# One exponential for the sinks of a pair of attention units, and sums by VectorE, on one Trainium2 core

## The reference, cut to what matters

```python
def window_attention(q, k, v, kc, vc, sink):
    ...
    logits = jnp.concatenate([s_win, s_ctx, _sink_column(sink, s_win)], axis=-1)
    p = jax.nn.softmax(logits, axis=-1)
    nw = 3 * BLOCK
    nc = kc.shape[1]
    o = (jnp.einsum('bnhgqk,bnkhd->bnqhgd', p[..., :nw].astype(v.dtype), vw)
         + jnp.einsum('bnhgqc,bchd->bnqhgd', p[..., nw:nw + nc].astype(v.dtype), vc))
```

## Time and profile before

| | us |
|---|---|
| median of 3 runs | 2042.43 |
| lowest and highest of the runs | 2041.19, 2049.43 |
| profiled execution, its time | 2047.0 |
| profiled execution, its span | 2045.2 |
| PE busy in the span | 1948.9 |
| DVE busy | 1232.9 |
| ACT busy | 941.1 |
| POOL busy | 491.1 |

### The profile page before, as it was taken

How to read it: one execution, slowest core, us unless ns; L and a number is a source line. 1 busy time by engine, 2 the same in 40 slices (tenths; PEclk the granted TensorE clock), 3 DMA queues, 4 the chain that set the end, 5 groups by cost and what they waited for, 6 DMA issues and landing times.

```text
span 2045.2 us, 30423 instructions
## 1 busy us (share of the span) xinstructions
PE 1948.9 (95%) x12246; PEld 1722.2 (84%) x12246; DVE 1232.9 (60%) x1914; ACT 941.1 (46%) x1490; POOL 491.1 (24%) x326
## 2 busy tenths in 40 slices
PE   7999898899989999999799999999999899999999
PEld 6899886899977888787588788888877898799999
DVE  4688796778855781653763583354365947676410
ACT  4454445555447333433753542233255454765643
POOL 1301022000000000000444544455510000303887
PEclk9999999899999999999999999999999999999999
DMA  6987472466832212221023244465523233144554
GB/s 234 282 303 257 160 256 74 164 237 217 268 110 87 72 52 72 83 83 62 11 93 111 105 151 148 144 200 201 192 87 103 93 118 131 63 148 153 185 189 151
DMA packets 84636, 299.23 MB, mean 146 GB/s; under 512 B 9992, under 2 KB 13200, under 8 KB 84112
## 3 DMA queue, kind: packets, MB, share of 16 engines
q1 hardware_dynamic: 64512, 231.76, 32.9%
q0 software_dynamic: 17280, 60.95, 9.3%
q10 hardware_dynamic: 2704, 4.57, 0.6%
HBM read 296.18 MB, written 4.11 MB: 147 GB/s over the span
## 4 chain that ended last, share of the span: by engine, by line
PE 81%; DVE 8%; ACT 5%; DMA 3%; issue 2%; POOL 1%; ACTq 0%; DVEq 0%; POOLq 0%
PE ps L458 23%; PE ps L453 23%; PE ps L456 23%; DVE wl L436 3%; DMA wr<-wstream 2%; PE ps L538 1%; PE ps L1638 1%; ACT wh L420 1%; PE ps L982 1%; PE ps L984 1%; PE ps L987 1%; PE ps L1055 1%; PE ps L1074 1%; PE ps L1093 1%; DVE K L1727 1%
## 5 line engine op out<-in xcount | busy, mean ns | idle before, releaser
L453 PE MATMUL ps<-HH,wh 128*128 128x256 f32 (+1 forms) x2336 | 765.3, 328 | 22.9 <-ACT HH L1357 10.7
L458 PE MATMUL ps<-HH,wl 128*128 128x256 f32 (+1 forms) x2336 | 753.4, 322 | 6.9 <-DVE wl L436 6.0
L456 PE MATMUL ps<-HL,wh 128*128 128x256 f32 (+1 forms) x2336 | 752.4, 322 | 1.1 <-DVE HL L1371 1.0
L420 ACT ACTIVATE wh<-wr 128x1024 fp32r<-128x1024 f32 x440 | 461.7, 1054 | 392.7 <-PE ps L458 338.7
L453 PEld LDWEIGHTS ps<-HH,wh 128*128 128x128 f32 x2336 | 449.1, 192 | 68.7 <-issue 29.9
L436 DVE TENSOR_TENSOR wl<-wr,wh 128x1024 fp32r<-128x1024 f32 x297 | 361.9, 1226 | 233.8 <-ACT wh L420 230.4
L458 PEld LDWEIGHTS ps<-HH,wl 128*128 128x128 f32 x2336 | 449.1, 192 | 42.4 <-DVE wl L436 8.8
L456 PEld LDWEIGHTS ps<-HL,wh 128*128 128x128 f32 x2336 | 449.1, 192 | 37.0 <-issue 2.4
L436 POOL TENSOR_TENSOR wl<-wr,wh 128x1024 fp32r<-128x1024 f32 x143 | 355.7, 2492 | 189.8 <-ACT wh L420 189.0
L1210 POOL TENSOR_TENSOR s<-s,ST 128x512 f32<-128x512 f32 x56 | 57.3, 1039 | 745.6 <-DVE ST L1178 745.0
L458 PE MATMUL ps<-HIDH,wl 128*128 128x512 f32 (+1 forms) x512 | 173.1, 338 | 0.0
(11 more groups left out here) (251 smaller groups left out, 2541.9 us busy)
## 6 DMA issues: line engine op xcount, KB each, us to landing
wr<-wstream SPq DMA_DIRECT2D x440, 512.0 KB, 3.3
WM<-wmod POOLq DMA_DIRECT2D x68, 512.0 KB, 3.8
X<-wmod POOLq DMA_DIRECT2D x28, 512.0 KB, 5.6
NAB<-naskew POOLq DMA_DIRECT2D x16, 128.0 KB, 12.3
dilskew<-lines POOLq DMA_DIRECT2D x1, 2048.0 KB, 20.7
DILB<-dilskew POOLq DMA_DIRECT2D x2, 1024.0 KB, 13.0
COND<-cond ACTq DMA_DIRECT2D x2, 1024.0 KB, 5.6
CT<-consts POOLq DMA_DIRECT2D x1, 1216.0 KB, 9.4
```

Of the source, the lines that this page charges most:

```text
L420: ins = e.activation(self.WH[i % NSPL][:, :], self.WR[n % NRAW][:, :], ACT.Copy)
L453: e.matmul(out, wh, xh, start=i == 0, stop=False)
L456: e.matmul(out, wh, xl, start=False, stop=False)
L458: ins = e.matmul(out, wl, xh, start=False, stop=i == n_k - 1)
```

## The change

The sinks' exponentials of both units of a pair are taken by one ACT instruction in place of two, after the first unit's exponentials. Since one instruction has one bias, DVE first adds the sinks to the negative maxima of both units (`dve_pair_diff`, a new instruction behind the pair's last negative maximum, ahead of the fill). The addition of the sink's exponential to the sum becomes a tensor-tensor addition, one a unit for either kind, in place of a tensor-scalar one a row. DVE's first sum of a pair waits for the pair's sink exponential (`u_sink`), and ACT's sink exponential waits for DVE's addition (`u_diff`).

```diff
@@ act_unit_exp
-        if u.kind != "b1":
-            ins = e.activation(st[:, 6:6 + rows], st[:, 2:2 + rows], ACT.Exp, bias=self.unit_sink(u, l))
         ins.then_inc(*self.c("u_exp").mark(u.key))
+
+    def pair_stats(self, pair, col):
+
+        at = self.st.item(pair[0].key)
+        return self.ST[:, at:at + 2, col:col + pair[0].rows]
+
+    def pair_sinks(self, pair, l):
+        v = self.unit_sink(pair[0], l)
+        return bass.AP(v.tensor, v.offset, [list(v.ap[0]), [pair[1].head - pair[0].head, 2], [0, pair[0].rows]])
+
+    def act_pair_sink(self, e, w, pair):
+        key, at = pair[1].key, self.pair_stats(pair, 6)
+        w.wait_ge(*self.c("u_diff").at(key))
+        e.activation(at, at, ACT.Exp).then_inc(*self.c("u_sink").mark(key))
+
+    def dve_pair_diff(self, e, w, pair, l):
+
+        for u in pair:
+            w.wait_ge(*self.c("u_neg").at(u.key))
+        ins = e.tensor_tensor(self.pair_stats(pair, 6), self.pair_stats(pair, 2), self.pair_sinks(pair, l), ALU.add)
+        ins.then_inc(*self.c("u_diff").mark(pair[1].key))
@@ act_units
                 self.act_unit_exp(e, w, u, S, l)
+                if u.kind != "b1" and u is pairs[t][0]:
+                    self.act_pair_sink(e, w, pairs[t])
@@ dve_unit_sum
         if u.kind != "b1":
-            for i in range(u.rows):
-                ins = e.tensor_scalar(den[:, i:i + 1], den[:, i:i + 1], st[:, 6 + i:7 + i], None, ALU.add)
+            w.wait_ge(*self.c("u_sink").at(pair[1].key))
+            ins = e.tensor_tensor(den, den, st[:, 6:6 + u.rows], ALU.add)
             ins.then_inc(*self.c("u_den").mark(u.key))
@@ dve_units
                 self.dve_unit_max(e, w, u, S, l)
+            if after and after[0].kind != "b1":
+                self.dve_pair_diff(e, w, after, l)
             fill()
```

More of the change, by code:

```diff
@@ L218 @@
     "cond", "m_ttr", "m_set",
-    "u_score", "u_side", "u_s", "u_max", "u_neg", "u_exp", "u_den", "u_inv", "u_p", "u_tr", "u_pt", "u_pv", "u_out",
+    "u_score", "u_side", "u_s", "u_max", "u_neg", "u_diff", "u_sink", "u_exp", "u_den", "u_inv", "u_p", "u_tr", "u_pt", "u_pv", "u_out",
     "o_v", "o_hi", "o_lo", "oh_hi", "oh_lo", "fh_hi", "fh_lo", "at_hi", "at_lo",
@@ L1166, in dve_unit_max, with dve_unit_sum @@
         ins.then_inc(*self.c("u_neg").mark(u.key))
-    def dve_unit_sum(self, e, w, u):
+    def dve_unit_sum(self, e, w, u, pair):
         st = self.ST[:, self.st.item(u.key), :]
@@ L1188, in dve_units @@
                 if 0 <= t < n:
-                    self.dve_unit_sum(e, w, pairs[t][i])
+                    self.dve_unit_sum(e, w, pairs[t][i], pairs[t])
                 if not both:
```

## The result

The changed kernel takes 2051.58 us in the median of 10 runs (2048.53 to 2054.97). The kernel before, run beside it and with its three earlier runs, takes 2046.48 us (10 runs, 2041.19 to 2049.43). The ratio is 1.0036, with a 95% interval of 1.0027 to 1.0045: slower by 7.4 us (5.5 to 9.2; the two medians are 5.1 us apart), less than the 0.5% taken as the bound of "same". The forecast was 2046.6 us. The direction was right; the time is 5.0 us above the forecast, just past the upper end of the range (2051.5).

What follows compares the result with a forecast made beforehand. PE was taken as the bound, except in 71 us where it waits for a DVE, ACT, POOL loop. Layer 0's 2.2 and 0.3 and layer 1's 1.7 make +4.2 us on 2042.43: 2046.6 us, range 2040.5 to 2051.5.

Steps and rivals of the forecast that it cites:

- the 71 us: Layers 0 and 1 after the gates' matmuls, 977 to 1021 and 1767 to 1794 us: only these can move.
- Step 1: ACT's sink exponentials: 20 of 40 go, ACT gains 0.19 us a pair and the second sum can start 0.19 earlier.
- Step 2: DVE's new addition takes 0.17 us after a 0.03 us wait; the fill and first sum start some 0.20 us later.
- Step 3: Tensor-tensor sums take 0.17 us, gaining alone 0.04 us a sum in x pairs and 0.17 in c pairs.
- Step 4: Second sums with two SBUF inputs wait for POOL's multiplication, ending 0.02 us after it; together +4.2 us, chance 0.68.
- held pairs: x pairs whose second exponentials end after POOL has started: five of six in layer 0, four of five in layer 1.
- The price of a held pair: A blocked x pair costs 0.48 us on POOL and 0.55 on DVE, taken as 0.5; 0.75 if DVE alone were the loop.
- A c pair: Layer 0's four c pairs: the blocked sum makes each 0.06 to 0.1 us slower, 0.3 us in all.
- the base: The time the sum was added to: the runs' median of 2042.43 us, 4.6 us below the profiled execution.
- No block: Sums run beside POOL unhindered or never overlap it: between -1.2 and +0.2 us, giving 2041.5; chance 0.20.
- held through both POOL instructions: DVE waits for both of POOL's instructions in 9 x and 4 c pairs: 17.7 us more, giving 2060; chance 0.03.
- The relief of ACT: Rival that ACT was the bound: 15 open pairs each gain 0.19 us, -2.9 in all, giving 2039.5; chance 0.05.

Runs made afterwards that it cites:

- scalar sums: The changed kernel with its sums in the old tensor-scalar form, one instruction a row; DVE's addition and the shared exponential stay: 2045.21 us, 1.0008.
- the addition alone: The kernel before plus DVE's addition of the sinks, into columns nobody reads; sums and exponentials as before: 2044.96 us, 1.0005.
- the writes: POOL writes a constant in place of multiplying in layers 0 and 1; with 8 pieces: changed kernel 2044.96 us (1.0007), kernel before 2046.01 (1.0006).
- the one-input multiplication: POOL's x-unit multiplication as tensor-scalar: changed kernel 2057.5 us (1.0075), kernel before 2051.24 (1.0048), changed kernel with tensor-scalar sums 2055.53 (1.0065).

## Why the prediction was right, and where it missed

**Where the time is.** Right. Nearly all of the loss (6.4 of the 8.0 us between the profiled executions) lies in the 71 us in which PE waits; the pairs under the gates' matmuls are hit by the hold as well (POOL sits idle for 0.29 us between its instructions at 964.38 and 965.70) and keep their distance to the hundredth.

**Step 1, ACT.** One of two sink exponentials is gone, as said, and the one that stays takes 0.21 us in place of 0.28 and holds ACT for 0.11 in place of 0.19, which wasn't forecast. ACT's relief shows no gain: scalar sums, which have it, are no shorter than the kernel with the addition alone (1.1 us of loss against 0.8 in the shorter lengths).

**Step 2, the addition.** Its 0.17 us was right (0.16). The wait for the result ahead of it was taken as 0.03 us from a place where one wait stands; it is 0.11 us here, and once 0.46. That made it 0.27 us a pair and not 0.20. ACT waits for it 8 times, 2.7 us in all, in most of them 0.3 us and once 0.64, above the 0.37 given as the bound:

```profile
987.86 0.21 ACT L1123 ACTIVATE ST<-ST 128x2 f32<-128x2 f32 x1 [0.64 <-DVE ST L1129]
```

The addition alone costs 1.1 us in the lengths, and the sum had it at nothing where POOL was idle in any case.

**Step 3, the sums' form.** Right: 0.14 to 0.16 us where 0.17 was put.

**Step 4, the hold.** Right in its mechanism, in its place and to 0.02 us in its end: 0.86 to 1.03 us for the held sums, 0.29 us between POOL's two instructions. The number of held pairs was wrong: 6 of 11 and not 9. In four pairs DVE is late by the pairs before, and both its sums start ahead of POOL. The fifth, the sixth x pair of layer 0, was counted by the end of its exponentials; but its second sum comes behind other work of DVE, and in the kernel before, too, it started when POOL had 0.07 us left:

```profile
999.28 0.20 DVE L1175 TENSOR_SCALAR ST<-ST 128x1 f32<-128x1 f32 x1
...
998.31 1.04 POOL L1210 TENSOR_TENSOR s<-s,ST 128x512 f32<-128x512 f32 x1 [1.57 <-DVE ST L1178]
```

The price of a held pair was about right: the three of layer 0 lost 0.59 us each where 0.5 was taken. The unheld pairs were put at nothing and lost 0.24 each, of which the addition alone explains some 0.1 (0.54 us for six pairs in its own kernel). A c pair costs 0.11 where 0.08 was put. Fewer held pairs and a loss in the others made up for each other, and that was luck: 2.9 us in layer 0 where 2.5 was forecast, and 1.9 without the clock in layer 1 where it was 1.7. The Trainium skill's rule (SBUF — State Buffer, "Who interferes with whom"), by which a DVE instruction with two SBUF inputs contends with a GpSimd instruction that reads SBUF and not with one that only writes it, agrees with the held sums and with the writes; for the one-input multiplication it would have the sum held for all of the 1.56 us, and the trace has 0.52 and 0.17.

**Why the time is outside the range.** Two terms failed. The first is the base: the forecast was added to 2042.43, the median of three runs whose spread was 8 us, and the kernel before has 2046.48 in the ten runs that the comparison rests on. The 4.6 us between the profiled execution and the median were read as chance; the clock's part in it was not looked for. The second is the clock: a loop that gets slower was costed at the full clock, and the profiled execution lost 2.1 us more while the granted clock was 0.50. No term of the sum stood for that, and the range's upper end had only 2 us for the spread of the runs. The base alone is 4.05 of the 5.0 us. But it isn't all: against the kernel before, the change costs 7.4 us (5.5 to 9.2) where 4.2 was forecast. In the two lengths the profiled execution has 4.8 without the clock's 1.56, so the units' own loss was sized within 0.6 us. Why the changed kernel's runs have the lower clock stays open. The base itself is uncertain by some us: beside the experiments the kernel before took 2043.98 (32 runs), 2041.45 (7) and 2043.49 (23). The upper end of the range is a near miss, too: its own terms, 2042.43 + 7.2 + 2, give 2051.6, and it was written as 2051.5.

**The rivals.** "No block" falls with the held sums, and "held through both POOL instructions" didn't occur: no sum is longer than 1.03 us. The relief of ACT exists but isn't where the time is.

No version that computes the right values beats the kernel before. The best of them, scalar sums with the shared exponential, isn't told apart from it.

## What to carry to other kernels

Before an element-wise instruction is rewritten from one tensor input to two, look at what GpSimd does at that moment: beside GpSimd's two-input multiplication the hold lasted until that instruction ended, so its price is set by GpSimd's tile and not by your own, and the smallest operation is hit hardest (0.16 us became 1.03). Count it in the pairs where it sits on the loop that ends last, and nothing elsewhere. Find these pairs by where the instruction itself starts, and not by the end of what it waits for. A loop that gets slower around TensorE should be given a term for the granted clock, and a base should be a median of runs whose clocks are known.

## What the runs showed of the hardware

- GpSimd's multiplication of 128x512 by a number a partition took 1.565 us as TENSOR_SCALAR and 1.040 us as TENSOR_TENSOR with the number broadcast. I had expected the form with one tensor input to be no slower.
- Beside that TENSOR_SCALAR a DVE addition with two SBUF inputs took 0.52 and 0.17 us, and ended well before GpSimd did. Beside the two-input multiplication of the same execution it was held to the end. Why it is held in part is open.
- A second collision came up that the prediction didn't have: once POOL's instructions move apart, the second meets other work. What it costs the kernel wasn't measured. At the end of layer 1 the fill L2141, 128x256, takes 1.16 us. It ends 0.27 us after POOL, and so did the one at this place before, which came later in POOL's work (1789.74 for 0.60 us, POOL's end at 1790.07); without POOL beside it the same fill takes 0.41 to 0.42.

```profile
1794.92 1.16 DVE L2141 TENSOR_TENSOR HL<-FR,HH 128x256 fp32r<-128x256 f32 x1 [0.23 <-ACT HH L2135]
...
1794.77 1.04 POOL L1233 TENSOR_TENSOR s<-s,ST 128x512 f32<-128x512 f32 x1 [0.29 <-DVE ST L1199]
```

- The mean granted clock of one and the same kernel, the kernel before, varies between 0.989 and 0.993 over 32 runs, and its time with it, from 2049.1 to 2038.8 us. Over the ten runs of the changed kernel (0.988 to 0.991) the time doesn't follow it.
